# Expert stages of a decoder trunk: gated rows added into DRAM sums by accumulating scatters, the shared expert run as passes of the same sequence

## The reference, cut to what matters

```
def moe(h, router_w, router_bias, w1, w3, w2, ws1, ws3, ws2):
    scores = sigmoid(xt @ router_w)                  # (T, 64)
    # group-limited top-k on scores + router_bias: 4 of 8 groups, then 8 experts
    gates = take_along_axis(scores, eidx)            # un-biased
    gates = gates / sum(gates) * 2.5
    for expert e, for its tokens tok:
        acc[tok] += gate * ((silu(x[tok] @ w1[e]) * (x[tok] @ w3[e])) @ w2[e])
    out = acc + (silu(xt @ ws1) * (xt @ ws3)) @ ws2  # one shared expert for all tokens
x = LN(ALPHA * x + (1 + gate_ada) * out)             # DeepNorm residual, gate from c
```

## Time and profile before

| | |
|---|---|
| Median of 3 runs | 2981.86 us (2980.83 to 2983.79) |
| The profiled execution | 2983.08 us, its span 2981.4 us |
| TensorE matmul busy | 2661.9 us, 89% of the span |
| VectorE, ScalarE, GpSimd busy | 1037.0, 628.8, 360.3 us |
| DMA | 658.03 MB, mean 221 GB/s |
| Mean granted TensorE clock | 0.944 of full speed |
| Stretch of the expert passes | about 900 to 1523 us (layer 0), 2253 to 2874 us (layer 1) |

### The profile page before, as it was taken

How to read it: one execution, slowest core, us unless ns; L and a number is a source line. 1 busy time by engine, 2 the same in 40 slices (tenths; PEclk the granted TensorE clock), 3 DMA queues, 4 the chain that set the end, 5 groups by cost and what they waited for, 6 DMA issues and landing times. The chain is left out here.

```text
span 2981.4 us, 31993 instructions
## 1 busy us (share of the span) xinstructions
PE 2661.9 (89%) x11495; PEld 1506.3 (51%) x11496; DVE 1037.0 (35%) x2058; ACT 628.8 (21%) x1263; POOL 360.3 (12%) x396
## 2 busy tenths in 40 slices
PE   6998989899859999999974999999868999999974
PEld 3565556556734444444432476676744444444431
DVE  1434334423361222221138444444352222221138
ACT  0112030311221211221111333433221112111211
POOL 0000001000001111111100122121101111111101
PEclk9999989999969999999986999999978999999987
DMA  6532416243157999999955121221257999999954
GB/s 260 163 109 87 136 49 182 69 127 96 36 224 273 364 382 387 384 378 389 373 228 170 39 83 44 71 70 36 73 197 276 357 386 393 381 385 381 372 236 181
DMA packets 180803, 658.03 MB, mean 221 GB/s; under 512 B 30408, under 2 KB 92200, under 8 KB 125376
## 3 DMA queue, kind: packets, MB, share of 16 engines
q1 hardware_dynamic: 129872, 525.43, 45.9%
q0 software_dynamic: 37632, 104.92, 10.1%
q10 hardware_dynamic: 13168, 25.89, 3.0%
HBM read 624.64 MB, written 60.85 MB: 230 GB/s over the span
## 5 line engine op out<-in xcount | busy, mean ns | idle before, releaser
L1662 PE MATMUL moe_py<-weights_w,moe_hT 128*128 128x512 f32 (+1 forms) x1040 | 375.9, 595 | 3.5 <-ACT moe_hT L1239 3.5
L1648 PE MATMUL moe_ph<-weights_w,moe_xT 128*128 128x512 f32 x832 | 373.4, 602 | 1.8 <-DVE moe_xT L1449 1.8
L1648 PE MATMUL moe_pr<-weights_w,moe_xT 128*64 128x512 f32 (+1 forms) x1248 | 369.7, 596 | 1.1 <-DVE moe_xT L1449 1.1
L862 PE MATMUL attn_proj<-core_hT,attn_w_w 128*128 128x512 f32 x768 | 341.4, 606 | 15.4 <-issue 12.9
L1449 DVE COPY moe_xT<-moe_tx 128x512 f32<-128x512 f32 x104 | 71.9, 691 | 752.1 <-PE moe_tx L1621 752.1
L862 PEld LDWEIGHTS attn_proj<-core_hT,attn_w_w 128*128 128x128 f32 x768 | 149.1, 195 | 201.1 <-issue 197.1
L1648 PEld LDWEIGHTS moe_ph<-weights_w,moe_xT 128*128 128x128 f32 x832 | 155.6, 192 | 179.8 <-issue 179.8
L1648 PEld LDWEIGHTS moe_pr<-weights_w,moe_xT 128*64 128x64 f32 (+1 forms) x1248 | 134.3, 154 | 194.7 <-issue 193.8
L2226 PE MATMUL gdn_pj<-core_hT,gdn_w_w 128*128 128x512 f32 x512 | 226.4, 596 | 0.0
L1290 POOL DMA_INDIRECT y_rows<-moe_ysb,moe_yidx x104 | 105.5, 1015 | 993.1 <-ACT moe_ysb L1248 850.7
L1662 PEld LDWEIGHTS moe_py<-weights_w,moe_hT 128*128 128x128 f32 (+1 forms) x1040 | 140.2, 169 | 163.6 <-issue 156.4
(11 more groups left out here) (366 smaller groups left out, 3018.4 us busy)
## 6 DMA issues: line engine op xcount, KB each, us to landing
weights_w<-in_expert_w_dram SPq DMA_DIRECT2D x384, 1024.0 KB, 12.0
attn_w_w<-in_attn_w_in_dram SPq DMA_DIRECT2D x36, 1024.0 KB, 8.7
weights_w<-y_rows SPq DMA_DIRECT2D x32, 1024.0 KB, 5.3
attn_ada_w<-in_ada_w_dram POOLq DMA_DIRECT2D x64, 384.0 KB, 5.9
gdn_w_w<-in_gdn_w_in_dram SPq DMA_DIRECT2D x16, 1024.0 KB, 6.0
normNone_w<-in_ada_w_dram SPq DMA_DIRECT2D x8, 1536.0 KB, 6.4
attn_swp<-attn_raw ACTq DMA_DIRECT2D x192, 64.0 KB, 2.1
gdn_ada_w<-in_ada_w_dram POOLq DMA_DIRECT2D x32, 384.0 KB, 3.6
```

The lines of the kernel that those rows point to most:

```text
L862: last = nc.tensor.matmul(proj[n % 2][:], w[:, j % SLOTS, kk, half_ * P:(half_ + 1) * P], c.hT[:, kk, :], start=kk == 0, stop=kk == KT - 1)
L1648: last = nc.tensor.matmul(ph[b][at, :], xT[:, b, k, at], w13[:, n % UP, :, k], start=k == 0, stop=k == KT - 1)
L1662: last = nc.tensor.matmul(py[n][at, :], hT2[:, b, k, at], w2[:, load % DOWN, k, half(n)], start=k == 0, stop=k == 1)
```

## The change

- The norm stage also computes the router's scores (`scores(t)`, TensorE, L566 of the new file) and their sigmoid, stores the normalised x as `x_rows`, loads the shared expert's weights into slots of their own and four experts instead of three.
- The gather takes rows of `x_rows`; `by` and `plus` are applied in the copies after the transposes, now four operations of 128x128 on each of ScalarE and VectorE instead of one copy of 128x512.
- The constants (iota, index tables, identity in bf16) are loaded from DRAM instead of being computed. The gates are computed for all experts in one step and travel through the index matmuls (7 columns instead of 5), so that each row's gate is at hand as `gcol`; ScalarE multiplies by it when it copies `py` to `ysb`.
- The scatter adds into DRAM: `sums` has two sums per token (1024 rows), which passes use in turn by the parity of their place, a pass of two experts one for each. It waits until earlier scatters into the same sums have landed. The sums are set to zero in the attention stage by 8 transfers of 1 MiB from DRAM to DRAM, ahead of everything else on SyncE's queue there.
- The shared expert's four tiles are items of the sequence: tiles 0 and 1 ahead of the first routed pass, between the routing's matmuls, tiles 2 and 3 behind the last. Their result is added to x at once (`merge`).
- The overflow bookkeeping is spread over passes 12 and 14 to 22. At the end 4 loads of 1 MiB bring the sums back, and VectorE does three operations per tile.

```
-FULL, DOUBLE, PASSES = 38, 3, 52
+EARLY, FULL, DOUBLE, PASSES = 4, 38, 4, 52
+SUMS = 2
+COLS = 7
...
 def expert_passes():
-    passes, ranks = [], []
+    seq, ranks, routed = [Pass(None, tile=0), Pass(None, tile=1)], [], 0
...
+    seq += [Pass(None, tile=t) for t in tiles]
...
 # mid_stage, sync
+            weights.load_router(sp)
+            weights.load_shared(sp)
+            weights.load_expert(sp, 0)
+            for t in range(TT):
+                sp.wait_ge(xn_ready, t + 1)
+                sp.dma_start(x_rows[t * P:(t + 1) * P, :], c.x[:, t]).then_inc(weights.x_out, 16)
+            for e in range(1, EARLY):
+                weights.load_expert(sp, e)
 # mid_stage, tensor
+            def scores(t):
+                pe.wait_ge(laid_act, t + 1)
+                pe.wait_ge(laid_dve, t + 1)
+                to = logits.rearrange("p k n -> p (k n)")[:, t * NE:(t + 1) * NE]
+                for k in range(KT):
+                    last = nc.tensor.matmul(to, c.hT[:, k, t * P:(t + 1) * P], weights.rw[:, k], start=k == 0, stop=k == KT - 1)
+                if t == TT - 1:
+                    last.then_inc(lg_done, 1)
...
 # attention_stage, sync
+            for s in sums:
+                for t in range(TT):
+                    sp.dma_start(s.rearrange("(t p s) d -> t p (s d)", p=P, s=SUMS)[t], zeros_dram.ap()).then_inc(cleared, 16)
             turn(0, True)
...
 # moe_stage, scalar
+            def turn_in(b):
+                for k in range(4):
+                    last = nc.scalar.activation(xT[:, b, k], tx[0][:, k], ACT.Identity, scale=by[:, k:k + 1], bias=plus[:, k:k + 1])
+                return last
...
+                        ins = nc.scalar.activation(ysb[:, i % 2, half(n)], py[n][:], ACT.Copy, scale=gcol[:, ps.p % 4:ps.p % 4 + 1])
...
 # moe_stage, gpsimd
             def scatter(b, s, done):
-                pool.indirect_dma_start(y_rows, bass.IndirectOffsetOnAxis(ap=yidx[:, s:s + 1], axis=0), ysb[:, b], None,
-                                        bounds_check=SEQ * TOPK - 1, oob_is_err=False).then_inc(done, 16)
+                pool.indirect_dma_start(sums[l], bass.IndirectOffsetOnAxis(ap=sidx[:, s:s + 1], axis=0), ysb[:, b], None,
+                                        bounds_check=SUMS * SEQ - 1, oob_is_err=False, compute_op=ALU.add).then_inc(done, 16)
...
+                for j in earlier(i):
+                    pool.wait_ge(y_out[j % 2], scattered(j))
+                scatter(i % 2, ps.p % 4, y_out[i % 2])
...
 # moe_stage, vector, in iteration p
+                if p is not None and p + 3 < PASSES:
+                    if p >= 1:
+                        before_p = seq.index(routed[p - 1])
+                        dve.wait_ge(y_out[before_p % 2], scattered(before_p))
+                    to_add((p + 3) % 4, idx_ready)
...
 # moe_stage, the end
+            for t in range(TT):
+                sp.dma_start(back[:, t], sums[l].rearrange("(t p s) d -> p t s d", p=P, s=SUMS)[:, t]).then_inc(sums_in[t], 16)
...
             for t in range(TT):
-                a = acc[:, t % 2]
-                for k in range(TOPK):
...
+                s = back[:, t, 0]
+                dve.wait_ge(sums_in[t], 16)
+                ch.do(nc.vector.tensor_tensor(s, s, back[:, t, 1], ALU.add))
+                ch.sync()
+                ch.do(nc.vector.scalar_tensor_tensor(out=s, in0=c.ada[:, 2], scalar=1.0, in1=s, op0=ALU.add, op1=ALU.mult))
+                ch.sync()
+                ch.do(nc.vector.tensor_tensor(c.x[:, t], c.x[:, t], s, ALU.add))
```

More of the change, by code:

```diff
@@ L548, in _ @@
                     last.then_inc(turned, 1)
+                if weights is not None and t:
+                    if t == 1:
+                        pe.wait_ge(weights.router_in, 64)
+                    scores(t - 1)
+            if weights is not None:
+                scores(TT - 1)
     st.close()
@@ L969, in take @@
         return len(ranks) - 1
-    while len(passes) < PASSES:
-        n = 0
[L973 to L980, removed]
+    tiles = iter(range(2, TT))
+    n = 0
+    while routed < PASSES:
+        want = EARLY if routed == 0 else 3
+        while n < want and len(ranks) < NE - 2:
+            r = next(ahead, None)
+            if r is None:
+                break
+            at = take(r)
+            seq.append(Pass(routed, [r], [at]))
+            routed, n = routed + 1, n + 1
+            if r == DOUBLE:
+                seq.append(Pass(routed, [r], [at], start=P))
+                routed, n = routed + 1, n + 1
+        n = 0
         a, b = next(behind), next(behind)
-        passes.append(Pass([a, b], [take(a), take(b)]))
+        seq.append(Pass(routed, [a, b], [take(a), take(b)]))
+        routed += 1
+    seq += [Pass(None, tile=t) for t in tiles]
     last = {}
-    for p, ps in enumerate(passes):
+    for i, ps in enumerate(seq):
         for n in ps.loads:
-            last[n] = p
-    return passes, ranks, last
+            last[n] = i
+    return seq, ranks, last
 class ExpertWeights:
-    EARLY = 3
     UP, DOWN = 4, 4
@@ new lines, in _ @@
+            silu(0)
+            act.wait_ge(gate_turned, 1)
+            nc.scalar.copy(gateT, gateT_ps).then_inc(gateT_ready, 1)
+            silu(1)
+            hidden(0)
+            rows_out(0)
+            hidden(1)
+            turned(0)
+            rows_out(1)
+            silu(2)
+            turned(1)
+            for i in range(2, ITEMS):
+                hidden(i)
+                if seq[i].p is not None and seq[i].p + 2 < PASSES:
+                    turned(seq[i].p + 2)
+                if i + 1 < ITEMS:
+                    silu(i + 1)
+                rows_out(i)
@@ L1432, in one_hots @@
             def one_hots(p):
-                ps = passes[p]
+                ps = routed[p]
                 for n, r in enumerate(ps.ranks):
@@ L1677, in _ @@
-            last.then_inc(lg_turned, 1)
+            routed = [(i, ps) for i, ps in enumerate(seq) if ps.p is not None]
+            up_of(0)
             pe.wait_ge(sel_ready, 1)
-            pe.wait_ge(consts, 4)
             for s in range(TT):
@@ L1732, in block @@
                 pe.wait_ge(ov["xTd"], j + 1)
-                up(ph[0], lambda k: xT[:, 0, k], SPARE_UP, ov["h"])
+                for k in range(KT):
+                    last = nc.tensor.matmul(ph[0][:], xT[:, 0, k], w13[:, SPARE_UP, :, k], start=k == 0, stop=k == KT - 1)
+                last.then_inc(ov["h"], 1)
                 pe.wait_ge(ov["hh"], j + 1)
@@ L1736, in block @@
                 pe.wait_ge(ov["hT"], j + 1)
-                down(0, SPARE_DOWN, ov["y"])
+                for n in range(2):
+                    for k in range(2):
+                        last = nc.tensor.matmul(py[n][:], hT2[:, 0, k], w2[:, SPARE_DOWN, k, half(n)], start=k == 0, stop=k == 1)
+                last.then_inc(ov["y"], 1)
                 pe.wait_ge(ov["out"], 16 * j + 16)
```

740 lines of the change are left out of this document (348 added, 392 removed).

## The result

The changed kernel takes 3020.88 us (median of 4 runs, 3013.74 to 3022.25) against 2982.82 us for the kernel before beside it: a ratio of 1.0119, 95% interval 1.0098 to 1.0141. It is slower by 1.2%, where 2952 us and a gain were forecast. Its profiled execution took 3013.74 us, the fastest of its four and 30.7 more than that of before; the traces can explain these 30.7 us, where the medians are 38 apart.

A forecast was written before the change was run, and what follows sets the result against it. It took TensorE as the bound in the passes, with DMA (share 0.96) and the scatter loop (1.1 us spare) just under it. Sum: 2983.1-76.4-9.4+4+51 = 2952 us; range 2893 to 3045.

The forecast's parts named there:

- The tail: After each layer's last routed down projection: 45.0 us would replace 84.1 and 82.3, a gain of 76.4 us together.
- The opening: Norm stage to first routed `up`: earlier router scores would gain 4.7 us per layer, 9.4 us in all.
- The clearing: Attention stage: zeroing transfers would delay the positions and mask and stall TensorE, costing 4 us, between 0 and 17.
- The passes: Routed expert passes: the adding scatter would make the loop late by about 0.55 us a pass, costing 51 us.
- The other way to count agrees: Check on the passes: DMA work of 12.0 us a pass, above the 11.63 us period, taken as agreeing with 0.55 us.
- The loop in the same term: Scatter, landing, index reduce, index matmuls: landing +1.5 us, reduce +0.16, less 1.1 spare, about 0.55 us late a pass.
- The signs: Profile marks named ahead: tail, first `up`, scatter landing, TensorE's `sidx` waits, pass period; also what would prove the prediction wrong.
- the middle case: Passes lose 0.1 to 0.8 us each: 2915 to 2976 us, landing about 10.4, period 12.2; chance 0.38.
- the bound scatter: Passes: the scatter's landing of 12.7 us sets the period, over 12.6 us; upper end of the range, 3045 us.
- The scatter becomes the bound: Rival on the passes: landing grows by 3.8 us, 1.5 us a pass stay, 138 us: 3040 us; chance 0.27 (over 2988).
- Adding is free: Rival on the passes: landing stays 8.9 us, only the extra reduce shows, some 3 us: 2904 us; chance 0.27.
- The rule: Skill text applied to the scatter: adding runs at about half the copy's rate, so engine time 0.87 becomes 1.74 us.

The follow-up runs named there:

- late_clear: Changed kernel with the clearing transfers behind the first and last turns of the attention stage instead of ahead of everything: 3004.78 us, ratio 1.0063 to the kernel before.
- less_weights: Changed kernel, still adding with 4 slots, loading only half of each expert's down weights from the fifth expert on: 2978.47 us, ratio 0.9963 to the kernel before.
- slots8_less: Changed kernel, adding, with 8 slots for row numbers and gates instead of 4, and half the down weights unloaded from the fifth expert on: 2903.63 us, ratio 0.9715.
- plain: Changed kernel with its scatter writing instead of adding, all waits kept: 2926.72 us, ratio 0.9796 to the kernel before.
- slots8_less_plain: Changed kernel with 8 slots instead of 4, half the down weights unloaded from the fifth expert on, and a writing scatter: 2903.69 us, ratio 0.9737.
- slots8_twice: Changed kernel with 8 slots instead of 4, each scatter writing, then writing the same rows again into another tensor: 3014.58 us, ratio 1.0072 to the kernel before.

## Why the prediction was wrong

The time lies inside the stated range, on the side that had a chance of 0.27; the sum and the direction were wrong.

- **The tail (-76.4): right.** It gave 77.7. The 45.0 us from the last routed `down` became 37.4, because the first shared `up` (7.0) ran ahead of that `down`; with it the sum is 44.4.
- **The opening (-9.4): right in sign, 5.5 in size.** The scores ended at 877.9, 23.4 us after the first transposes, for 23.6 in the forecast. But the second tile's transposes came at 861.96, 7.5 us behind the first for 5.6 before, and the expert stage's first matmul stood at 880.59, 2.7 us after the scores.
- **The clearing (+4, 0 to 17): mis-sized, 12.1.** What failed here is how late the tables come. I had the loads in flight beside 8 MiB and let them lose a little. The positions landed in 5.3 us, but the table of 1 KB took 22.0 us and the mask 34.7 (3.6 and 6.3 before), and VectorE waited 21.95 us for the table (3.0 in `late_clear`). 18 us late less the 6.28 of slack is 12, which the same sentence of the forecast would have given. The 12.1 count from the start of the launch; the attention stage itself, from its first projection to the norm stage, lost 14.1, and what lies ahead of it was 2.0 us shorter. The profiled run of `late_clear`, the slowest of its four, got back 7 of the 14; the rest I put down to the granted clock, which was lower in it (0.90 from 700 to 800 for 0.98 in the changed kernel), and did not test.
- **The passes (+51): the step that failed.** It is "The other way to count agrees: (0.96x11.63+0.87) us of DMA work a pass is 12.0 us, above 11.63." The engine time that I added, 0.87, is what the runs show (0.84), but two things beside it were wrong. I compared the work with a share of 1, and over 1000 to 1400 no run here has a share above 0.96 (single stretches of 100 us reach 0.99); the kernel before was at 0.96 already. And 11.63 us was one pass; the mean of that window is 11.96. Done properly, from the same trace: 0.96 x 11.96 = 11.5 us of work a pass, with 0.84 more 12.3, at a share of 0.96 a period of 12.8; measured 12.80. That is 0.84 us a pass and 77 in 92 passes, and some 2978 us for the sum as a whole, within the 6 us that the prediction itself calls none. I took the second count for a check on the first; it was a second limit, and the higher one.
- **What no term had.** 77 us are not 102.5. From 1400 to the last `up` the period of layer 0 is 13.5 us, with TensorE waiting for weights ahead of all four passes of two experts. And 27.4 of the 102.5 us, in both layers, are TensorE's matmuls at the lower clock: behind some of its waits an `up` took 8.6 us (after 2.19, at 1390.67) or 9.7 (after 5.58, at 1565.91) in place of 7.1. Whether the passes would have been shorter at full clock, or TensorE's waits longer, no run shows.
- **The loop in the same term** ("late by 1.5+0.16-1.1") was about right in its parts and too cheap as a whole. The landing grew by 1.8 us for 1.5, and TensorE waited 30.9 us for it in layer 0 where 25 were forecast. But where the loop is the limit left, in `less_weights` against `slots8_less`, it costs 75 us, with 24.8 us of such waits in layer 0 and a granted clock of 0.98 for 1.00.
- **The signs** named ahead were mixed: the landing (10.7) and TensorE's waits (30.9) were those of the middle case, the period (12.8) that of the bound scatter. So the loop alone did not set the period. GpSimd did stand waiting for landings, 28.2 us in 3 waits, which was to be a sign of being wrong; `slots8_less`, where it waits 121.6 us, shows that this cost nothing.
- **The rivals.** "The scatter becomes the bound", 3040 us, was on the right side, by the wrong mechanism: the landing was 10.7 and not 12.7, and opening the loop gained 8 us. "Adding is free" fails with `plain`; it would hold in a kernel whose DMA and whose loop have room, as `slots8_less` against `slots8_less_plain` shows.
- **The rule.** The Trainium skill ("Collectives: The Full Stack", the section on why AG, RS and AR differ) says of rings of three or more ranks that ReduceScatter, which adds, gets about half the rate of AllGather, which copies, because the add needs two source reads. For a scatter into DRAM this case's trace agrees with the half: 1.71 against 0.87 us of engine time, and one adding transfer weighs as two writes in `slots8_twice`. That it is a second source read that costs, no row here shows.

What stays open: why the share of the DMA engines settles at 0.95, and falls to 0.92 from 1400 to 1500, while TensorE waits for weights. Passes of two experts adding to one sum only, which would spare some of the scatters' waits, were not tried: the same token can be in both halves.

## What to carry to other kernels

Where two resources are near full, work out each one's period from its own share and take the higher, with the period and the share from the same window and not from one pass. The share to compare with is the one that such a kernel reaches, here 0.95 to 0.96 over 400 us; from there on extra engine time lengthened the period one for one (0.84 us of it, 0.84 us a pass). The list of waits names who came last, not what would bind if he were gone: before you cure the wait that it names, ask what is level with it, and test the two cures alone and together. Work that needs only the idle engine belongs inside the stretch that the other resource bounds, not at its end.

## What the hardware showed that I had not expected

- Adding to DRAM takes twice the engine time of writing (1.71 against 0.87 us for a scatter) but lands only 1.8 us later under load (10.7, 8.9) and 2.4 at light load (7.7, 5.3). The landing is a poor measure of what a transfer takes from others.
- GpSimd issues an adding scatter in 1.66 us, a writing one in 1.02 (means of 31 and 33 from 1000 to 1400, changed kernel and before).
- Loads issued on ScalarE's queue just after 8 MiB of DRAM-to-DRAM transfers on SyncE's fared very differently: a table of 1 KB landed in 22.0 us (3.6 before) and the mask of 1 MiB in 34.7 (6.3), but the positions of 256 KB, issued first, in 5.3 (2.8).
